# Two modulation parts moved from beside the second mixer to beside the fourth

## What is computed

```python
mod = silu(c) @ ada_w + ada_b                 # 1024 -> 6 x 1024
sh1, sc1, g1, sh2, sc2, g2 = split(mod, 6)
h = rmsnorm(x, norm_mix_w) * (1 + sc1) + sh1
proj = h @ w_in                               # four mixers' columns, and 4 x 1024 gate columns
merged = sum(sigmoid(gate_n) * (y_n @ w_branch[n]) for n in 4 mixers)
x = x + g1 * (merged @ w_out)
h = rmsnorm(x, norm_ffn_w) * (1 + sc2) + sh2
x = x + g2 * ((silu(h @ w_gate) * (h @ w_up)) @ w_down)
```

## Time and profile before

| | |
|---|---|
| runs | 2385.4, 2396.78, 2396.56 us; median 2396.56 |
| profiled execution | 2382.31 us, span of the trace 2380.2 us |
| TensorE busy | 2259.4 us, 95% |
| VectorE / ScalarE / GpSimd busy | 44% / 29% / 41% |
| granted TensorE clock, mean | 0.977 |
| RWKV, from the first scores to the third chunk, layer 0 | 318 to 388 us |
| retention, layer 0 | 598 to 697 us |

### The profile page before, as it was taken

The page is one execution under the profiler, slowest core; times in us unless marked ns, Lnnn a source line. Parts: engine busy times, 40 slices in busy tenths (PEclk is TensorE's granted clock), DMA queues, the critical chain, the costliest instruction groups (busy, mean ns, idle before and its releaser), DMA issues. The chain is left out here.

```text
span 2380.2 us, 47018 instructions
## 1 busy us (share of the span) xinstructions
PE 2259.4 (95%) x20560; PEld 2097.7 (88%) x20560; DVE 1045.1 (44%) x1520; ACT 692.2 (29%) x885; POOL 987.7 (41%) x1166
## 2 busy tenths in 40 slices
PE   6989988999999999999989899899899999999997
PEld 3978977988989999999979699679888999999997
DVE  4174766675554511111133756766564444111112
ACT  3345221311233322222234352232121323222221
POOL 0532421352545445554443233125434564555453
PEclk8999989999999999999999999999999999999998
DMA  7332121111333243322234322211123332222221
GB/s 284 124 135 78 67 99 64 45 63 50 134 110 118 72 142 126 107 89 89 89 138 136 120 77 79 73 66 63 45 100 116 103 121 70 91 89 96 83 97 72
DMA packets 68460, 233.41 MB, mean 98 GB/s; under 512 B 10784, under 2 KB 11296, under 8 KB 67872
## 3 DMA queue, kind: packets, MB, share of 16 engines
q1 hardware_dynamic: 61344, 214.88, 26.5%
q10 hardware_dynamic: 6912, 15.53, 1.8%
HBM read 219.03 MB, written 11.35 MB: 97 GB/s over the span
## 5 line engine op out<-in xcount | busy, mean ns | idle before, releaser
L753 POOL TENSOR_TENSOR ring_lo<-ring,w_hi 128x256 fp32r<-128x256 f32 x1104 | 887.5, 835 | 1103.3 <-ACT w_hi L1473 1047.6
L828 PE MATMUL gm<-H_hi,ring_lo 128*128 128x260 f32 x3328 | 694.8, 290 | 11.5 <-POOL ring_lo L753 4.8
L828 PE MATMUL gm<-H_lo,w_hi 128*128 128x260 f32 x3328 | 682.9, 286 | 0.7 <-issue 0.7
L828 PE MATMUL gm<-H_hi,w_hi 128*128 128x260 f32 x3328 | 679.3, 285 | 0.5 <-issue 0.5
L828 PEld LDWEIGHTS gm<-H_hi,ring_lo 128*128 128x128 f32 x3328 | 520.3, 190 | 46.4 <-issue 14.3
L828 PEld LDWEIGHTS gm<-H_lo,w_hi 128*128 128x128 f32 x3328 | 517.6, 190 | 7.6 <-issue 5.9
L828 PEld LDWEIGHTS gm<-H_hi,w_hi 128*128 128x128 f32 x3328 | 516.2, 189 | 5.9 <-issue 4.8
L1473 ACT ACTIVATE w_hi<-ring 128x1024 fp32r<-128x1024 f32 x256 | 270.5, 1056 | 453.2 <-PE gm L828 174.7
L1385 PE MATMUL gm<-AF_hi,ring_lo 128*128 128x260 f32 x704 | 142.1, 283 | 2.2 <-DVE AF_lo L2516 2.2
L2521 DVE TENSOR_TENSOR AT<-gm,GT 128x520 f32<-128x520 f32 x44 | 30.8, 700 | 256.0 <-ACT GT L1780 256.0
L2451 DVE TENSOR_SCALAR Y<-gm,MOD 128x520 f32<-128x520 f32 x32 | 24.3, 759 | 267.4 <-PE gm L1385 220.4
(11 more groups left out here) (399 smaller groups left out, 2809.1 us busy)
## 6 DMA issues: line engine op xcount, KB each, us to landing
ring<-wall SPq DMA_DIRECT2D x372, 512.0 KB, 3.3
WB<-wbranch SPq DMA_DIRECT2D x32, 256.0 KB, 3.6
xsave<-X SPq DMA_DIRECT2D x2, 2080.0 KB, 12.1
X<-xsave ACTq DMA_DIRECT2D x8, 520.0 KB, 5.2
arena<-states ACTq DMA_DIRECT2D x8, 512.0 KB, 3.9
sst<-arena ACTq DMA_DIRECT2D x8, 512.0 KB, 2.7
X<-xt SPq DMA_DIRECT2D x1, 2080.0 KB, 12.2
y<-H SPq DMA_DIRECT2D x4, 520.0 KB, 2.7
```

The source lines that it names most:

```text
L753: ins = pool.tensor_tensor(ring_lo[:, SLOT[i], k], ring[:, SLOT[i], k], hi[:, k].bitcast(F32), ALU.subtract)
L828: ins = pe.matmul(out[:, hf, 0:HALF], w[a][:, k, :], src[b][:, k, HALF * hf:HALF * (hf + 1)], start=first and a == "lo", stop=last and a == b)
```

## The change

The two parts that stood beside RW stand beside RT, which then has four. All eight gates of gated DeltaNet now have a half part in front. The numbers in `GIVEN` are set so that every gate stays behind the stage where it stood; with it go the half parts and turns. `FILL_AT` is unchanged.

```diff
-PARTS_BESIDE = {HG: 4, RW: 2, GD: 0, RT: 2}
+PARTS_BESIDE = {HG: 4, RW: 0, GD: 0, RT: 4}
...
-         RT: [1, 3, 1, 4, 1, 0, 0, 1, 1, 2, 0]}
+         RT: [2, 8, 0, 5, 0, 0, 0, 2, 0, 3, 0]}
```

More of the change, by code:

```diff
@@ L93 @@
 AT_BANK = {("ada", 0, 18): 18, ("proj", 1, 2): 18, ("proj", 2, 0): 12}
-PARTS_BESIDE = {HG: 4, RW: 2, GD: 0, RT: 2}
+PARTS_BESIDE = {HG: 4, RW: 0, GD: 0, RT: 4}
 DIAGONAL = 5
 GIVEN = {HG: [1, 1, 4, 1, 1, 0, 2, 0, 3, 0, 0, 2, 0, 1, 1, 0, 1, 2, 0],
-         RW: [1, 1, 1, 2, 2, 1, 1, 1, 1, 1, 1, 1, 1, 0, 1, 0, 1, 0, 1, 1, 0, 0, 2, 0, 0, 1, 1, 0],
+         RW: [1, 1, 1, 2, 2, 1, 1, 1, 1, 1, 1, 0, 1, 0, 0, 0, 1, 0, 0, 0, 0, 0, 1, 0, 0, 1, 0, 0],
          GD: [1, 1, 0, 1, 0, 1, 1, 1, 1, 1, 0, 1, 0, 0, 1, 0, 1, 1, 0, 0, 0, 1, 1, 1, 1, 0],
-         RT: [1, 3, 1, 4, 1, 0, 0, 1, 1, 2, 0]}
+         RT: [2, 8, 0, 5, 0, 0, 0, 2, 0, 3, 0]}
 FILL_AT = {HG: [22, 22, 30, 46, 30, 30, 30, 38, 30, 30, 14, 30, 30, 0, 8, 8, 8, 30, 26],
```

## The result

The changed kernel takes 2437.14 us (median of 4 runs, 2433.4 to 2438.7) against 2395.92 for the kernel before on the same chip: ratio 1.0204, 95% interval 1.0174 to 1.0234. The two medians lie 41 us apart, which by itself would be a ratio of 1.0172; on another chip (`a_again`) the medians of 4 and 14 runs lie 49 us apart, at a ratio of 1.0207. So the loss is 41 to 49 us. The forecast was 2422, and its range ended at 2438. The profiled execution took 2438.70 us with a span of 2436.6, so profiled against profiled it is 56.4 us, where the sum of the prediction had 33.5.

The account below looks back on a forecast made before the run. TensorE, busy 95% of the span, was taken to bound the kernel. Retention +30, RWKV -0.5 and the clock behind retention's gaps +4 gave +33.5 us on 2382.3, so 2416, plus 6 towards the median: 2422 us, range 2403 to 2438.

Parts of the forecast that it names:

- +4 us: Retention, both layers: half clock behind its two long gaps, 1 us for each, four in all.
- reaches L1142 where it did, within 1 us: RWKV: chunk 0 starts at L1142 unmoved within 1 us, as VectorE's lead behind the inverse is spent on gate 6.
- Rotation of q: Retention: it follows the third mixer's sums at once and waits for ScalarE, +1.2 us a layer.
- Transposes to scores: Retention: VectorE needs 7.7 us, TensorE has 3.8 us for it; 3.2 us more idle time a layer.
- Chunk 1 to L1112: Retention: chunk 1, scores and chunk 2 follow each other without gate 6 as fill, +2.4 us a layer.
- the work: Four half parts and two turns moved into retention, paid there in full: 5.2 us a layer.
- the sums: Retention, chunk 3 to the sums: no gate 7 matmuls between them any more, +3.0 us a layer.
- my theory (1): Formed after the result: retention's gaps come from the two-product limit; more than half of the miss there is the clock.
- I added 6 us: Profile to median: 6 of the 14 us by which the profiled execution lay below the median, taking 2416 to 2422 us.
- the gaps stay covered: Rival: retention's four gaps do not open, only work moves; 2390 to 2394 us, chance 0.08.
- RWKV regains the clock for nothing: Rival: first two chunks at half clock in both layers before, in none after; 2410 us or 2404, chance 0.16.
- The third: Rival: the clock falls in everything emptied, RWKV +17 us, retention's four gaps 2.8 each; 2440 us, chance 0.16.

Follow-up runs that it names:

- a_again: The changed kernel, unaltered, run again on the same chip as the run with both remedies: ratio 1.0207 to the kernel before.
- e1_due_early: Changed kernel with retention's half parts ahead of gates 4, 6 and 7 falling due one stage earlier: ratio 1.0084 to the kernel before.
- e2_rt_busy: Changed kernel with stand-in matmuls in three of retention's gaps, 18 of them ahead of the sums: ratio 1.0156 to the kernel before.
- e4_rw_busy: Changed kernel with stand-in matmuls in RWKV's waits at the scores and the inverse, both pairs of chunks: ratio 1.0155 to the kernel before.
- b1_busy: Kernel before with stand-in matmuls in RWKV's two long waits (27 in the 6.62 us, 10 in the 2.57 us): ratio 1.0007 to the kernel before.

## Why the prediction was right in kind and too small

The step that failed is the price of the clock behind what the change empties: the "+4 us" for retention's gaps, and in RWKV chunk 0 that "reaches L1142 where it did, within 1 us". Of the 22.9 us that the sum missed on the profiled execution (56.4 against 33.5), 11.7 lie in retention, 8.8 in RWKV and 2.3 in the third mixer.

- *Right: what opens and why.* All four gaps of retention came, and `e1_due_early` shows their cause to be the two-product limit. Rotation of q: 1.22 us (forecast 1.2). Transposes to scores: 2.68 and 0.60 (3.2 more). Chunk 1 to L1112: 0.53, 1.40 and 0.29 to 0.69 (2.4). Layer by layer the idle time grew by 10.8 and 11.2 us, forecast 9.8. With the work it is some 34 us in two layers instead of 30. The bounds of 24 to 34 were added up too narrowly: the terms named there, each at its end, give 23 to 36.
- *Too small: the sums.* I took 3.0 us behind chunk 3, from where L2109 ended before. But before, VectorE did its step for gate 6 (L2493, at 675.36) while TensorE was at L1112; now gate 6 begins behind L1112, and VectorE's steps for chunk 3 queue behind that gate's (the first row is of the kernel before, the others are of the changed one):

```profile
675.36 0.70 DVE L2493 SCALAR_TENSOR_TENSOR GT<-GT,gm 128x520 f32<-128x520 f32 x1 [0.18 <-ACT GT L1737]
...
695.56 0.70 DVE L2493 SCALAR_TENSOR_TENSOR GT<-GT,gm 128x520 f32<-128x520 f32 x1 [11.39 <-PE gm L862]
696.29 0.42 DVE L2050 TENSOR_TENSOR arena<-SM,CD 128x256 f32<-128x256 f32 x1
...
701.29 1.77 DVE L2109 TENSOR_TENSOR arena<-arena 128x1040 f32<-128x1040 f32 x1
```

 From the start of L2493 to the end of L2109 it is 7.5 us in both kernels, and TensorE now has 3.3 us for it (half part and chunk 3). The wait is 4.57.
- *Too small: the work.* 5.2 us a layer by the rows, 6.1 by TensorE's busy time at full clock (`e1_due_early`).
- *Mis-sized most in retention: the clock, +4 us for both layers together.* By busy time it cost 110.88 - 103.35 = 7.5 us in layer 0 and 107.12 - 103.40 = 3.7 in layer 1, together 11.2; by the length that `e2_rt_busy` saves, 6.5 and 2.4, together 8.9. I had taken 1 us for each of four gaps, between one price of 2.8 and one of 0.7, where the runs have 2.2 to 2.8. In one layer of each execution a part of it lies behind the 1.40 us wait at chunk 2 (L1112 3.78 us), a place that I had priced at nothing. The Trainium skill, TensorE: Matmul & The Clock Gate (§ HAM oscillation — how this bites in real kernels), says that a burst behind a stall is paid at half rate. By it the prediction named 7 us more for these gaps, and the trace agrees: 5 to 7. So the clock is about half of the 11.7 us missed in retention, as my theory (1) has it by busy time, not by length.
- *Mis-sized most in RWKV: chunk 0's start, "where it did, within 1 us".* It came 4.9 and 4.5 us later behind L1082. I had counted 1 us a layer for gate 6 behind the emptied inverse; but the whole inverse and, in layer 0, the first 8 of the gate's 24 L828 rows ran at half clock (0.57 in the row at 335.30): those 8 rows took 3.6 us instead of 1.9, and the inverse, at nothing in my sum, most of the rest. `e4_rw_busy` at full clock has +0.8 there. The other terms held: -6.96 us for layer 0's chunks (forecast -6.85), the third chunk's start with its scores +2.7 and +2.8 (+2.2). In layer 1 the half clock lasted into the third chunk, another 1.2 us that the sum did not have. The full clock in both layers' chunks was right, and the gate ahead of them paid for most of it: in layer 0 it is 0.2 us in all, and layer 1, which had no half clock in its chunks to win back, lost 8.1.
- *The step from the profile to the median.* I added 6 us because the profiled execution of before lay 14 below its median. The changed kernel's profile lies 1.6 us above its own median, and before ranged from 2374 to 2399 us on the chips used, the changed kernel from 2433 to 2440. So the 6 us brought the forecast nearer to the result by luck: they stand for nothing that the changed kernel was seen to do. Whether the wider spread is RWKV's clock in layer 1, as `b1_busy` shows that it can fall there, stays open.
- *The rivals.* That the gaps stay covered, and that RWKV regains the clock for nothing, have both fallen. The third, with the clock falling in everything that is emptied (2440), named the mechanism, though layer 0's chunks did not fall. That its number comes so near is luck in part: it has 17 us for RWKV, which lost 8.3, and less than was measured for the gaps, the work and the third mixer.

## What to carry to other kernels

Where an engine may run ahead by a fixed number of units, a small unit in front of a large one closes the window: it must fall due a stage earlier, or the place behind it has no fill (three half parts due a stage earlier were worth 29 us here). Price a new gap with the stretch behind it at half clock, and look for the next stretch with little work before calling a stretch at half clock won: here it came back elsewhere in the thin part. Stand-ins paid where they covered most of the thin part (12 us in RWKV of the changed kernel), and gave nothing where they filled its one long wait (the kernel before).

## What the runs showed of the hardware

- The same retention code took 120.3 us at a granted clock of 0.96 or 123.6 at 0.93 in the two layers of one execution, and in the other order of layers in the next.
- Behind the unfilled gap of 4.6 us L1015 took 3.8 us in all ten layers of five profiled executions, and 1.92 behind the 18 stand-ins.
- Waits of 0.5 to 1.4 us in a row, as around chunk 2, left the clock at full or took it to half (L1112 at 1.98 or 3.78 us) from one layer to the next, in the same code.
